# A tenth weight place for the experts, in the room of a smaller descriptor scratch, on one Trainium2 core

## The chip, the cores and the metric

The kernel runs on one core of one Trainium2 chip. The metric is the device time of one execution in microseconds (us); the median of three runs of the kernel before is 1637.58 us. A smaller number is better.

## The reference, cut to what matters

The work is two blocks on 256 tokens of width 1024, all in float32. The first block has two layers with retention, dilated attention, a gated mix and a feed-forward part of width 2816. The second has a state-space branch, a pooling branch and a mixture of 32 experts. The change touches how weights and small vectors arrive; the part whose weights it touches most is the mixture:

```python
MOE_EXPERTS = 32; MOE_TOP_K = 2; D_EXPERT = 512
def swiglu(xb, wg, wu, wd):
    return (jax.nn.silu(xb @ wg) * (xb @ wu)) @ wd
# each token goes to 2 of the 32 experts:
#   yb = swiglu(tokens of expert e, w_eg[e], w_eu[e], w_ed[e])
#   y  = sum over the token's experts of yb * gate weight
```

Each expert has three weights of 1024 x 512 (or 512 x 1024) float32 values, 2 MB (2,097,152 bytes) each, so 96 weights have to come from memory, 201 MB in all. All 32 experts are computed, each for at most 64 tokens.

## The kernel before, in words

The five engines run programs that are written out by hand, with semaphores between them. `weights()` makes one list of units of weights for both layers and the first part of the second block. SyncE (SP) loads them in order into the places of `ring` (four in the layers, two after), by `load_to(u)`, which waits until the unit that held the place has been split. ScalarE makes the high part of each quarter (`hi_to`), VectorE or GpSimd (POOL) the low part (`lo_to`), TensorE (PE) multiplies three times per quarter. PE signals `split_done`, and the splits of quarter k wait for it at quarter k - 4.

The stages follow each other: layer 0, layer 1, `convolution`, `scan` (32 steps over the 16 units called "merged"), `gates` (units "u", "branch_a", "branch_b", "out2"), `routing`, and then `experts`.

In `experts`, PE goes through 16 pairs of experts. For pair p it needs weights 6p to 6p + 5: two gate weights, two up weights, two down weights. `gate_up(p)` multiplies 64 columns for each expert of the pair with 512 columns of weights, `down(p)` does the product back. Weight k lies in `slot_for(0, k)`, which is `expert_slots[k % 9]`: four places in the arena, four in `ring`, one in `rows`, 2 MB each. Weights 0 to 7 are issued by ScalarE during `gates` as places come free. SP issues weight 8 when the last `out2` product has been read, and then, in `expert_loads(0, 8)`, the others in order: weight k waits until PE has signalled that it is done with weight k - 9 (`("gu", r, b, 0)` after the gate part, `("gu", r, b, 1)` after the up part, `("oe", r, b, 1)` after the down part). Weights 2, 9, 10 and the last four are loaded in halves (`half_load`). There are further rounds for experts with more than 64 tokens, behind a condition (`further`); they use eight places.

GpSimd issues small loads itself, 128 partitions wide as a rule: `c1`, `WS` (the gating weights, 128 x 4 runs of 512 bytes, at step k = 1 of each layer), `GB` (two gains, at k = 4), and at the very start `posi`, six pieces of `colrow`, two more, and then `GCOL`, `BCOL` (128 x 2 runs of 16 bytes each) and `BP` (128 x 4 runs of 16 bytes). A generator `small_loads()` holds 17 more. Two of them are issued at k = 8 of layer 0, the others one at a time after each `low(m)` of layer 0's steps m = 2 to 16; ten of those are the router's weights `WR` (128 x 4 short runs each). A step m of the feed-forward part is two quarters of weights: POOL makes `low(m)`, one low part of a quarter (the other is VectorE's), and this one load.

The descriptors of the loads that GpSimd issues lie in a scratch in the on-chip memory, at its default size in the kernel before (the argument `dynamic_dma_scratch_size` is not given).

Of the kernel before, what the change touches and what calls it, by code (L numbers as in the profile page):

```python
# [13 lines left out]
P = 128  # L14
D = 1024
# [276 lines left out]
def program(nc, A, out):  # L292
    st = ExitStack()
    with st:
# [24 lines left out]
        posi = sb("posi", [P, 2], I32)  # L319
        rope = sb("rope", [P, 2, 2, 32])  # L320
        rt = rows[:, 4 * D:4 * D + P].rearrange("p (a b c) -> p a b c", a=2, b=2)
        posf = sb("posf", [P, 2])
        cnt = sb("cnt", [P, 1], I32)
        AR = 26624
        ar_at = nc.sbuf_base + (-nc.sbuf_base) % 32
# [46 lines left out]
        s_last = {e: sem(f"last_{e}") for e in ("dve", "pool")}  # L372
        s_w = [[sem(f"expert{i}") for i in range(9)]] + [[sem(f"expert{r}_{i}") for i in range(8)] for r in range(1, ROUNDS)]
        s_second = [sem(f"expert_second{i}") for i in range(4)]
        s_round = [None] + [{e: sem(f"round{r}_{e}") for e in ("pe", "act", "dve")} for r in range(1, ROUNDS)]
# [55 lines left out]
        GT2 = view(23424, 2, 512)  # L431
        JUNK = view(25472, 2, 512)
        ACH = view(4096, 22, 256, rounded=True)
        ACL = view(9728, 22, 256, rounded=True)
# [53 lines left out]
        def blocks8(a0, a1, rounded=False):  # L488
# [43 lines left out]
        SEL, RK, CW, RS, CM, CB = R(400, 2, 32), R(464, 2, 32), R(528, 2, 32), R(592, 2, 32), R(656, 1, 2), R(660, 2, 36)  # L532
        expert_slots = [ar[:, 18432:18432 + SLOT], ar[:, 22528:22528 + SLOT], ar[:, 10240:10240 + SLOT], ar[:, 14336:14336 + SLOT],
                        ring[:, 0:SLOT], ring[:, SLOT:2 * SLOT], ring[:, 2 * SLOT:3 * SLOT], ring[:, 3 * SLOT:4 * SLOT], rows[:, D:D + SLOT]]

        slot_for = lambda r, k: expert_slots[k % (9 if r == 0 else 8)]

# [49 lines left out]

        in_halves = lambda r, k: r == 0 and (k in (2, 9, 10) or k >= 92)

        def half_load(e, k, q):  # L590

            p, j = divmod(k, 6)
            o = slot_for(0, k)[:, q * RAW:(q + 1) * RAW]
            w = A["w_expert_up_2" if j < 4 else "w_expert_down_2"][0, 2 * p + j % 2]
            src = w.rearrange("(q p k) n -> q p (k n)", q=2, k=4)[q] if j < 4 else w.rearrange("(p q k) n -> q p (k n)", q=2, k=2)[q]
            e.dma_start(o, src).then_inc(*landed(s_second[k % 4] if q else s_w[0][k % 9], ("ew", 0, k, q)))

        def tensor(t):  # L600
# [346 lines left out]
            def convolution():  # L947
# [17 lines left out]
                for m in range(24):  # L965
                    c = CHUNKS[m]
                    if m < 3:
                        finished(m + 1)
                    else:
                        bk = take(("cv", m), ("conv", m))  # L970
                        chunk(bk if c < 20 else bk[:, 256:512], q0 + 1 + m, 0 if c < 20 else 1, 2).then_inc(*sig(s_mm, ("cv", m), ("split_done", q0 + 1 + m)))
                    if m >= 2:
                        to_tokens(m - 2)
                    if m == 1:
                        bk = take(("dtt",), ("dtraw",))
                        t.wait_ge(*at("cv", -1, "kept"))
                        for i in range(4):
                            made = t.transpose(bk[:, i * 64:(i + 1) * 64], DTT[:, tok(i)], ident[0:64, 0:64])
                        made.then_inc(*sig(s_turn, ("dtt",)))
                    if m == 10:  # L980
                        dt_sums()
                    if m == 11:
                        bk = take(("acst",), ("acsr", 0), ("acsr", 1))
                        t.wait_ge(*at("acs"))
                        for i in range(4):
                            made = t.transpose(bk[:, tok(i)], ACS[:, i % 2, :], ident)
                        made.then_inc(*sig(s_turn, ("acst_t",)))
                    if m == 17:
# [12 lines left out]
                    if m in SUMMED:  # L1001
                        state_sum(SUMMED[m])
# [395 lines left out]
        def scalar(s):  # L1398
# [356 lines left out]
            def gates():  # L1755
                n0 = first["u",][1]
                for u in range(2):
# [4 lines left out]
                    if u == 0:  # L1762
# [11 lines left out]
                s.wait_ge(*at("sacc", 15))  # L1774
                expert_load(s, 0, 1)
                s.wait_ge(*at("ss", "kept"))
# [15 lines left out]
                for u in range(4):  # L1792
                    for a in range(2):
                        hi_to(n0 + 2 * u + a + 4)
                    if u >= 2:
                        s.wait_ge(*at("ba", 3))
                        half_load(s, 2, u - 2)
# [4 lines left out]
                expert_load(s, 0, 3)  # L1802
                s.wait_ge(*at("bb", 3, "kept"))
                expert_load(s, 0, 5)
                for n in range(1, 5):
                    s.wait_ge(*at("lo", len(quarters) - n))
                expert_load(s, 0, 4)
# [908 lines left out]
        def gpsimd(g):  # L2716
# [34 lines left out]
            def small_loads():  # L2751
# [13 lines left out]
                yield  # L2765
                for q in range(2):
                    rows_of = lambda x: x[512 * q:512 * q + 512].rearrange("(p k) n -> p k n", k=4)
                    g.dma_start(WR[:, 4 * q:4 * q + 4, 0:4], rows_of(A["w_router_group_2"][0])).then_inc(*landed(s_small[5]))
                    yield
                    for k in range(4):  # L2770
                        g.dma_start(WR[:, 4 * q:4 * q + 4, 4 + 8 * k:12 + 8 * k], rows_of(A["w_router_expert_2"][0, k])).then_inc(*landed(s_small[6]))
                        yield

            def layer(l):
# [9 lines left out]
                for k in range(28):  # L2784
                    lo_to(n0 + k + 4)
                    if k == 1:
                        g.wait_ge(*at("z", l, 0, 1))
                        g.wait_ge(*at("hl", j, 1, 1))
                        g.wait_ge(*at("hh", j, 1, 1))
                        g.dma_start(WS[:, :, :], A["w_s"][l].rearrange("g t s -> t g s")).then_inc(*landed(s_ws, ("ws_in", l)))  # L2790
                    if k == 4:
# [4 lines left out]
                    if k == 8 and l == 0:  # L2796
                        loads = small_loads()
                        next(loads), next(loads)
# [86 lines left out]
            g.dma_start(colrow[0:48, 2, :], fl(A["b_ada_2"][0])).then_inc(*landed(s_col[1]))  # L2885
            for o, name in ((GCOL, "ln1_g_2"), (BCOL, "ln1_b_2")):
                g.dma_start(fold(o, 2), A[name][0].rearrange("(q p k) -> p q k", q=2, k=4)).then_inc(*landed(s_col[3]))
            g.dma_start(fold(BP, 4), A["b_ada_2"][0][3 * D:5 * D].rearrange("(u p k) -> p u k", u=4, k=4)).then_inc(*landed(s_col[3], ("bp_in",)))
            layer(0)
# [73 lines left out]
        def sync(y):  # L2963
# [25 lines left out]
            def expert_loads(r, first_one):  # L2989

                n_slots = len(s_w[r])
                for k in range(first_one, 96):
                    if k >= n_slots and not (r == 0 and k in (9, 10)):
                        b, i = divmod(k - n_slots, 6)
                        y.wait_ge(*(at("gu", r, b, i // 2) if i < 4 else at("oe", r, b, 1)))
                    if not in_halves(r, k):
                        expert_load(y, r, k)
                    elif k == 10:
                        for q in range(2):
                            y.wait_ge(*at("gu", 0, 0, 0 if q else "first"))  # L3000
                            for x in (9, 10):
                                half_load(y, x, q)
# [5 lines left out]
            for l in range(2):  # L3008
# [5 lines left out]
                for m, u in ADA_AT[l].items():  # L3014
# [84 lines left out]
```

## Time and profile before

| what | value |
|---|---|
| median of 3 runs (lowest, highest) | 1637.58 us (1637.37, 1638.76) |
| span of the profiled execution, first to last instruction | 1635.8 us |
| TensorE busy, and its mean granted clock | 1585.8 us (97%), 0.995 |
| VectorE, ScalarE, GpSimd busy | 762.6, 611.0, 473.7 us |
| moved by DMA | 397.87 MB, mean 243 GB/s |

The span leaves out what lies ahead of the first and behind the last instruction, which is 1.8 us between the span and the median. Engine names in the rows: PE is TensorE's matmuls, PEld its weight loads, DVE VectorE, ACT ScalarE, POOL GpSimd, SP SyncE; a "q" behind one is its queue or sequencer. L145 and L151 are lines of helpers through which all matmuls and all two-tensor operations go, L171 is the one through which all loads go, so instructions are told apart by their tiles. Idle time of an engine stands in square brackets with what ended it.

### The profile page before, as it was taken

What the parts mean: (1) busy time and instruction counts of PE and PEld (TensorE: products, weight loads), DVE (VectorE), ACT (ScalarE), POOL (GpSimd) and SP (SyncE); (2) the same over time, 40 slices, a digit from 0 to 9 for tenths busy, and PEclk for the clock granted to TensorE, in tenths of its full rate; (3) what the DMA queues carried; (4) which work ended last, traced back from release to release, by engine and by line L of the source; (5) the groups of instructions that cost most, each with busy time, mean ns of one, the idle gap of its engine ahead of it and who ended that gap; (6) DMA issues with size and microseconds to landing.
All of it is one profiled execution on the core that took longest, in us unless ns stands there. A gap on an engine that the chain in (4) does not pass through costs nothing.

```text
span 1635.8 us, 24320 instructions
## 1 busy us (share of the span) xinstructions
PE 1585.8 (97%) x9881; PEld 1204.8 (74%) x9881; DVE 762.6 (47%) x1261; ACT 611.0 (37%) x1113; POOL 473.7 (29%) x305
## 2 busy tenths in 40 slices
PE   6999999999999999999999999999999999999997
PEld 5988899878889998888778888898644444444442
DVE  4554433246454332578776666446532323333223
ACT  4644444345544443555446665333211111111010
POOL 4342655433434444300036665343300000000000
PEclk9999999999999999999999999999999999999998
DMA  7654997546439986433313333957999999999995
GB/s 264 220 158 128 266 260 232 174 141 218 153 98 312 263 269 220 118 80 85 103 52 104 104 103 120 296 152 264 360 400 423 425 420 422 424 422 424 421 422 210
DMA packets 244757, 397.87 MB, mean 243 GB/s; under 512 B 6837, under 2 KB 195697, under 8 KB 223392
## 3 DMA queue, kind: packets, MB, share of 16 engines
q1 hardware_dynamic: 237840, 365.45, 64.6%
q10 hardware_dynamic: 3776, 20.85, 3.2%
q0 software_dynamic: 3024, 9.95, 1.8%
q8 instruction: 81, 1.33, 0.3%
q14 instruction: 36, 0.29, 0.1%
HBM read 395.17 MB, written 1.05 MB: 242 GB/s over the span
## 4 chain that ended last, share of the span: by engine, by line
PE 82%; DMA 9%; DVE 3%; issue 2%; ACT 2%; POOL 1%; ACTq 0%; DVEq 0%; POOLq 0%; SPq 0%
PE ps L145 80%; DMA arena<-in_w_expert_up 4%; DMA arena<-in_w_expert_gate 4%; PE ps L147 2%; DVE arena L151 1%; DVE arena L155 1%; DMA ring<-in_w_out 1%; POOL split_r L151 1%; ACT arena L149 1%; DMA X<-in_x 1%; ACT split_r L149 1%; DVE split_r L151 0%; DMA ring<-in_w_in 0%; POOL arena_r L151 0%; DVE X L155 0%
## 5 line engine op out<-in xcount | busy, mean ns | idle before, releaser
L145 PE MATMUL ps<-arena_r,split_r 128*128 128x256 f32 (+1 forms) x2984 | 459.9, 288 | 2.2 <-POOL split_r L151 2.2
L151 POOL TENSOR_TENSOR split_r<-ring,split_r 128x1024 fp32r<-128x1024 f32 (+1 forms) x142 | 329.3, 2320 | 304.2 <-ACT split_r L149 275.6
L145 PEld LDWEIGHTS ps<-arena_r,split_r 128*128 128x128 f32 x2984 | 393.3, 188 | 19.7 <-issue 13.6
L149 ACT ACTIVATE split_r<-ring 128x1024 fp32r<-128x1024 f32 (+1 forms) x293 | 295.7, 1019 | 265.2 <-PE ps L145 183.2
L151 DVE TENSOR_TENSOR split_r<-ring,split_r 128x1024 fp32r<-128x1024 f32 (+1 forms) x151 | 217.4, 1442 | 302.6 <-ACT split_r L149 302.4
L145 PE MATMUL ps<-split_r,arena_r 128*128 128x512 f32 (+1 forms) x1520 | 341.0, 378 | 4.1 <-POOL split_r L151 2.4
L145 PEld LDWEIGHTS ps<-split_r,arena_r 128*128 128x128 f32 x1520 | 276.1, 189 | 50.3 <-issue 7.1
L145 PE MATMUL ps<-arena 128*64 128x512 f32 (+8 forms) x1456 | 299.1, 461 | 6.3 <-DMA arena<-in_w_expert_gate 2.2
L145 PE MATMUL ps<-hhh_r,split_r 128*128 128x256 f32 (+1 forms) x976 | 221.7, 316 | 0.0
L145 PEld LDWEIGHTS ps<-arena 128*64 128x64 f32 (+2 forms) x1456 | 126.0, 148 | 129.7 <-issue 115.2
L145 PE MATMUL ps<-ring,arena 128*64 128x512 f32 (+2 forms) x768 | 211.4, 576 | 3.0 <-DMA ring<-in_w_expert_up 1.7
L149 ACT ACTIVATE arena<-ps 128x256 f32<-128x256 f32 (+4 forms) x175 | 75.4, 446 | 257.3 <-PE ps L145 215.3
L145 PEld LDWEIGHTS ps<-hhh_r,split_r 128*128 128x128 f32 x976 | 161.6, 188 | 12.5 <-issue 0.6
L151 DVE TENSOR_TENSOR arena<-arena,ps 128x512 f32<-128x512 f32 (+1 forms) x120 | 72.7, 634 | 202.9 <-PE ps L145 177.3
L145 PEld LDWEIGHTS ps<-ring,arena 128*64 128x64 f32 (+1 forms) x768 | 77.3, 144 | 98.8 <-issue 89.4
L171 POOL DMA_DIRECT2D rows<-in_ln_g x1 | 0.6, 617 | 412.2 <-PE ps L145 412.2
L149 ACT ACTIVATE arena<-ps,modc 128x128 f32<-128x128 f32 x80 | 30.0, 455 | 199.2 <-PE ps L145 198.5
L149 ACT ACTIVATE arena_r<-arena 128x512 fp32r<-128x512 f32 (+2 forms) x96 | 51.0, 540 | 138.5 <-DVE arena L155 86.9
L145 PEld LDWEIGHTS ps<-arena,X 128*128 128x128 f32 x640 | 77.4, 198 | 28.5 <-issue 26.4
L145 PE MATMUL ps<-arena,X 128*128 128x128 f32 x640 | 82.6, 284 | 14.6 <-DVE arena L153 14.6
L155 DVE SCALAR_TENSOR_TENSOR arena<-ps,rows,arena 128x508 f32<-128x508 f32 (+4 forms) x104 | 69.7, 675 | 28.5 <-ACT arena L149 21.9
L151 POOL TENSOR_TENSOR arena_r<-arena,arena_r 128x256 fp32r<-128x256 f32 (+1 forms) x46 | 38.1, 830 | 151.3 <-ACT arena_r L149 143.7
(164 smaller groups left out, 1234.0 us busy)
## 6 DMA issues: line engine op xcount, KB each, us to landing
ring<-in_w_gate_up SPq DMA_DIRECT2D x88, 512.0 KB, 7.4
arena<-in_w_expert_gate SPq DMA_DIRECT2D x15, 2048.0 KB, 27.9
ring<-in_w_in SPq DMA_DIRECT2D x57, 512.0 KB, 5.3
ring<-in_w_expert_gate SPq DMA_DIRECT2D x13, 2048.0 KB, 25.7
ring<-in_w_expert_down SPq DMA_DIRECT2D x13, 2048.0 KB, 28.5
arena<-in_w_ada SPq DMA_DIRECT2D x24, 1024.0 KB, 7.4
arena<-in_w_expert_up SPq DMA_DIRECT2D x12, 2048.0 KB, 25.1
ring<-in_w_down SPq DMA_DIRECT2D x22, 1024.0 KB, 4.9
```

Source lines behind the costliest of these rows:

```text
L145: made = e.matmul(*a, **k)
L147: made = e.transpose(*a, **k)
L149: made = e.activation(*a, **k)
L151: made = e.tensor_tensor(*a, **k)
L155: made = e.scalar_tensor_tensor(**k)
L171: made = e.dma_start(*a, **k)
```

## The change

1. `dynamic_dma_scratch_size=512` is given: the descriptors' scratch takes 512 bytes of each partition. In the room there is a new tensor `tenth` of 2 MB. The small table `rope` moves into the arena.
2. `expert_slots` has ten places in the first round, `tenth` being the first. Weight k lies in place k % 10. What ScalarE issued as weights 0 to 7 it now issues as weights 1 to 8, at the same points and into the same places. Weight 0 is issued by SP in the scan, after eight units of "merged", and goes into `tenth`. After the last `out2` product SP issues weight 9, and weight k then waits until PE is done with weight k - 10. The weights in halves are now 3, 10, 11 and the last four.
3. GpSimd's loads of 512 runs are each cut in two of 256: `WS` is loaded at k = 1 and k = 3 of each layer, `BP` in two, each `WR` load in two (20 in place of 10). `GCOL`, `BCOL` and `BP` move from the start into the generator, ahead of `WR`. The generator now holds 31 loads; two are issued at k = 8 of layer 0, and one after each `low(m)` in both layers: 20 in layer 0 (m = 2 to 21), 9 in layer 1 (m = 2 to 10).

```diff
-        rope = sb("rope", [P, 2, 2, 32])
+        tenth = sb("tenth", [P, SLOT])
...
+        rope = ar[:, 26496:26624].rearrange("p (a b c) -> p a b c", a=2, b=2)
...
-        expert_slots = [ar[:, 18432:18432 + SLOT], ar[:, 22528:22528 + SLOT], ...
+        expert_slots = [tenth[:, :], ar[:, 18432:18432 + SLOT], ar[:, 22528:22528 + SLOT], ...
-        slot_for = lambda r, k: expert_slots[k % (9 if r == 0 else 8)]
+        slot_for = lambda r, k: expert_slots[k % (10 if r == 0 else 8)]
-        in_halves = lambda r, k: r == 0 and (k in (2, 9, 10) or k >= 92)
+        in_halves = lambda r, k: r == 0 and (k in (3, 10, 11) or k >= 92)
...
-                        t.wait_ge(s_small[5], 32)
-                        t.wait_ge(s_small[6], 128)
+                        t.wait_ge(s_small[5], 64)
+                        t.wait_ge(s_small[6], 256)
...
-                        expert_load(s, 0, 0)
+                        expert_load(s, 0, 1)
...
-                expert_load(s, 0, 6)
                 expert_load(s, 0, 7)
+                expert_load(s, 0, 8)
...
+                for o, name in ((GCOL, "ln1_g_2"), (BCOL, "ln1_b_2")):
+                    g.dma_start(fold(o, 2), ...)
+                    yield
+                for x in range(2):
+                    g.dma_start(fold(BP, 4)[:, 2 * x:2 * x + 2, :], ...)
+                    yield
-                for q in range(2):
+                for q in range(4):
                     (one load of WR[:, 2q:2q+2, 0:4], four of WR[:, 2q:2q+2, 4+8k:12+8k], a yield after each)
...
-                        g.dma_start(WS[:, :, :], A["w_s"][l].rearrange("g t s -> t g s")).then_inc(...)
+                    if k in (1, 3):
+                        x = k // 2
+                        g.dma_start(WS[:, 2 * x:2 * x + 2, :], A["w_s"][l, 2 * x:2 * x + 2].rearrange("g t s -> t g s")).then_inc(...)
...
-                    if l == 0:
-                        next(loads, None)
+                    next(loads, None)
...
-            for o, name in ((GCOL, "ln1_g_2"), (BCOL, "ln1_b_2")):
-                g.dma_start(fold(o, 2), ...)
-            g.dma_start(fold(BP, 4), ...)
...
+            load_to(first["merged",][0] + 8)
+            expert_load(y, 0, 0)
             load_to(first["end",][0])
             y.wait_ge(*at("o2", 1, 1, "kept"))
-            expert_loads(0, 8)
+            expert_loads(0, 9)
...
-    nc = bacc.Bacc("TRN2", target_bir_lowering=False, num_devices=1)
+    nc = bacc.Bacc("TRN2", target_bir_lowering=False, num_devices=1, dynamic_dma_scratch_size=512)
```

## Rows read from the trace of the kernel before

**Rows 1.** The page: busy time, and GB/s in 40 slices of the span.

```profile
PE 1585.8 (97%) x9881; PEld 1204.8 (74%) x9881; DVE 762.6 (47%) x1261; ACT 611.0 (37%) x1113; POOL 473.7 (29%) x305
...
GB/s 264 220 158 128 266 260 232 174 141 218 153 98 312 263 269 220 118 80 85 103 52 104 104 103 120 296 152 264 360 400 423 425 420 422 424 422 424 421 422 210
```

**Rows 2.** Windows: stretch, its length, busy time of each engine, clock, DMA share, GB/s.

```profile
890.00:960.00 70.00, 70.00 (x541) 60.85 (x538) 42.95 (x88) 42.99 (x98) 41.53 (x23) 1.00 0.40 105
...
1172.00:1196.00 24.00, 24.00 (x146) 11.43 (x144) 6.71 (x12) 4.79 (x11) 7.72 (x6) 1.00 0.91 346
1196.00:1423.00 227.00, 227.00 (x1230) 104.81 (x1228) 74.38 (x135) 30.19 (x73) 0.00 (x0) 1.00 1.01 420
1423.00:1612.00 189.00, 179.75 (x950) 84.92 (x946) 56.37 (x97) 22.78 (x55) 1.14 (x2) 1.00 1.01 421
```

**Rows 3.** Waits of PE from 1160 to 1636: us in total, times, longest.

```profile
PE ps L145 <- DMA ring<-in_w_expert_gate: 3.3, 3, 1.3
PE ps L145 <- DMA arena<-in_w_expert_gate: 2.2, 2, 1.2
PE ps L145 <- DMA arena<-in_w_expert_up: 2.0, 3, 0.8
...
PE ps L145 <- DMA ring<-in_w_expert_up: 1.7, 2, 0.9
```

**Rows 4.** Timeline of PE in the experts: start, us, idle before it.

```profile
1473.40 0.61 PE L145 MATMUL ps<-arena 128*64 128x512 f32 x1 [0.99 <-DMA ring<-in_w_expert_gate]
...
1592.89 7.09 PE L145 MATMUL ps<-arena 128*64 128x512 f32 x32 [1.23 <-DMA arena<-in_w_expert_gate]
```

**Rows 5.** Timeline of SP's queue as the experts start.

```profile
1172.56 0.34 SPq L171 DMA_DIRECT2D arena<-in_w_expert_up  x1
...
1195.95 0.38 SPq L171 DMA_DIRECT2D ring<-in_w_expert_gate  x1
```

**Rows 6.** The chain that ended last, its piece at 1592.89.

```profile
1592.89 18.24 PE ps L145 x76
```

**Rows 7.** The scan: SP's loads from 899 on, and one of ScalarE's splits.

```profile
899.11 31.36 SPq L171 DMA_DIRECT2D ring<-in_w_in  x8
...
920.52 1.05 ACT L149 ACTIVATE split_r<-ring 128x1024 fp32r<-128x1024 f32 x1
```

**Rows 8.** Timeline of POOL, feed-forward steps: with a load, without, and layer 1.

```profile
219.80 0.74 POOL L151 TENSOR_TENSOR arena_r<-arena,arena_r 128x256 fp32r<-128x256 f32 x1 [1.95 <-ACT arena_r L149]
220.49 0.77 POOL L171 DMA_DIRECT2D small<-in_w_router_expert  x1
...
225.65 0.73 POOL L151 TENSOR_TENSOR arena_r<-arena,arena_r 128x256 fp32r<-128x256 f32 x1 [1.95 <-ACT arena_r L149]
...
271.67 0.74 POOL L151 TENSOR_TENSOR arena_r<-arena,arena_r 128x256 fp32r<-128x256 f32 x1 [2.42 <-ACT arena_r L149]
...
277.43 0.73 POOL L151 TENSOR_TENSOR arena_r<-arena,arena_r 128x256 fp32r<-128x256 f32 x1 [2.41 <-ACT arena_r L149]
...
502.21 2.39 POOL L151 TENSOR_TENSOR split_r<-ring,split_r 128x1024 fp32r<-128x1024 f32 x1 [0.21 <-ACT split_r L149]
506.55 0.74 POOL L151 TENSOR_TENSOR arena_r<-arena,arena_r 128x256 fp32r<-128x256 f32 x1 [1.94 <-ACT arena_r L149]
```

**Rows 9.** Timeline of PE as the feed-forward steps start: layer 0, layer 1.

```profile
169.03 3.11 PE L145 MATMUL ps<-arena_r,split_r 128*128 128x256 f32 x24 [0.83 <-POOL split_r L151]
...
502.56 6.01 PE L145 MATMUL ps<-arena_r,split_r 128*128 128x256 f32 x48
```

**Rows 10.** POOL's loads: KB each, median us from issue to landing.

```profile
arena<-in_w_s POOLq DMA_DIRECT2D x2, 256.0 KB, 7.0
...
small<-in_w_router_expert POOLq DMA_DIRECT2D x8, 16.0 KB, 5.8
```

**Rows 11.** Timeline of POOL behind the gains' loads at k = 4, layer 0 and layer 1.

```profile
43.03 1.84 POOL L151 TENSOR_TENSOR split_r<-ring,split_r 128x768 fp32r<-128x768 f32 x1 [1.75 <-ACT split_r L149]
...
378.68 1.83 POOL L151 TENSOR_TENSOR split_r<-ring,split_r 128x768 fp32r<-128x768 f32 x1 [4.90 <-ACT split_r L149]
```

More of the change, by code:

```diff
@@ L372, in program @@
         s_last = {e: sem(f"last_{e}") for e in ("dve", "pool")}
-        s_w = [[sem(f"expert{i}") for i in range(9)]] + [[sem(f"expert{r}_{i}") for i in range(8)] for r in range(1, ROUNDS)]
-        s_second = [sem(f"expert_second{i}") for i in range(4)]
+        s_w = [[sem(f"expert{i}") for i in range(10)]] + [[sem(f"expert{r}_{i}") for i in range(8)] for r in range(1, ROUNDS)]
+        s_second = [sem(f"expert_second{i}") for i in range(5)]
         s_round = [None] + [{e: sem(f"round{r}_{e}") for e in ("pe", "act", "dve")} for r in range(1, ROUNDS)]
@@ L532, in program @@
         SEL, RK, CW, RS, CM, CB = R(400, 2, 32), R(464, 2, 32), R(528, 2, 32), R(592, 2, 32), R(656, 1, 2), R(660, 2, 36)
-        expert_slots = [ar[:, 18432:18432 + SLOT], ar[:, 22528:22528 + SLOT], ar[:, 10240:10240 + SLOT], ar[:, 14336:14336 + SLOT],
+        expert_slots = [tenth[:, :], ar[:, 18432:18432 + SLOT], ar[:, 22528:22528 + SLOT], ar[:, 10240:10240 + SLOT], ar[:, 14336:14336 + SLOT],
                         ring[:, 0:SLOT], ring[:, SLOT:2 * SLOT], ring[:, 2 * SLOT:3 * SLOT], ring[:, 3 * SLOT:4 * SLOT], rows[:, D:D + SLOT]]
-        slot_for = lambda r, k: expert_slots[k % (9 if r == 0 else 8)]
+        slot_for = lambda r, k: expert_slots[k % (10 if r == 0 else 8)]
         ADA_AT = ({4: 0, 8: 1, 12: 2, 16: 3, 20: 4}, {3: 5, 6: 6, 9: 7, 12: 8, 15: 9, 18: 10, 20: 11})
@@ L595, in half_load @@
             src = w.rearrange("(q p k) n -> q p (k n)", q=2, k=4)[q] if j < 4 else w.rearrange("(p q k) n -> q p (k n)", q=2, k=2)[q]
-            e.dma_start(o, src).then_inc(*landed(s_second[k % 4] if q else s_w[0][k % 9], ("ew", 0, k, q)))
+            e.dma_start(o, src).then_inc(*landed(s_second[k % 5] if q else s_w[0][k % 10], ("ew", 0, k, q)))
         def tensor(t):
@@ L1774, in gates @@
                 s.wait_ge(*at("sacc", 15))
-                expert_load(s, 0, 1)
+                expert_load(s, 0, 2)
                 s.wait_ge(*at("ss", "kept"))
@@ L1796, in gates @@
                         s.wait_ge(*at("ba", 3))
-                        half_load(s, 2, u - 2)
+                        half_load(s, 3, u - 2)
                     s.wait_ge(*at("mt", u))
@@ L1801, in gates @@
                 s.wait_ge(*at("bb", 3))
-                expert_load(s, 0, 3)
+                expert_load(s, 0, 4)
                 s.wait_ge(*at("bb", 3, "kept"))
-                expert_load(s, 0, 5)
+                expert_load(s, 0, 6)
                 for n in range(1, 5):
                     s.wait_ge(*at("lo", len(quarters) - n))
-                expert_load(s, 0, 4)
+                expert_load(s, 0, 5)
                 s.wait_ge(*at("o2", 1))
-                expert_load(s, 0, 6)
                 expert_load(s, 0, 7)
+                expert_load(s, 0, 8)
             def routing():
@@ L2765, in small_loads @@
                 yield
-                for q in range(2):
-                    rows_of = lambda x: x[512 * q:512 * q + 512].rearrange("(p k) n -> p k n", k=4)
-                    g.dma_start(WR[:, 4 * q:4 * q + 4, 0:4], rows_of(A["w_router_group_2"][0])).then_inc(*landed(s_small[5]))
+                for o, name in ((GCOL, "ln1_g_2"), (BCOL, "ln1_b_2")):
+                    g.dma_start(fold(o, 2), A[name][0].rearrange("(q p k) -> p q k", q=2, k=4)).then_inc(*landed(s_col[3]))
+                    yield
+                for x in range(2):
+                    g.dma_start(fold(BP, 4)[:, 2 * x:2 * x + 2, :], A["b_ada_2"][0][(3 + x) * D:(4 + x) * D].rearrange("(u p k) -> p u k", u=2, k=4)).then_inc(
+                        *landed(s_col[3], *([("bp_in",)] if x else [])))
+                    yield
+                for q in range(4):
+                    rows_of = lambda x: x[512 * (q // 2):512 * (q // 2) + 512].rearrange("(p k) n -> p k n", k=4)[:, 2 * (q % 2):2 * (q % 2) + 2, :]
+                    g.dma_start(WR[:, 2 * q:2 * q + 2, 0:4], rows_of(A["w_router_group_2"][0])).then_inc(*landed(s_small[5]))
                     yield
                     for k in range(4):
-                        g.dma_start(WR[:, 4 * q:4 * q + 4, 4 + 8 * k:12 + 8 * k], rows_of(A["w_router_expert_2"][0, k])).then_inc(*landed(s_small[6]))
+                        g.dma_start(WR[:, 2 * q:2 * q + 2, 4 + 8 * k:12 + 8 * k], rows_of(A["w_router_expert_2"][0, k])).then_inc(*landed(s_small[6]))
                         yield
+            loads = small_loads()
             def layer(l):
@@ L2789, in layer @@
                         g.wait_ge(*at("hh", j, 1, 1))
-                        g.dma_start(WS[:, :, :], A["w_s"][l].rearrange("g t s -> t g s")).then_inc(*landed(s_ws, ("ws_in", l)))
+                    if k in (1, 3):
+                        x = k // 2
+                        g.dma_start(WS[:, 2 * x:2 * x + 2, :], A["w_s"][l, 2 * x:2 * x + 2].rearrange("g t s -> t g s")).then_inc(
+                            *landed(s_ws, *([("ws_in", l)] if x else [])))
                     if k == 4:
@@ L2796, in layer @@
                     if k == 8 and l == 0:
-                        loads = small_loads()
                         next(loads), next(loads)
@@ L2885, in gpsimd @@
             g.dma_start(colrow[0:48, 2, :], fl(A["b_ada_2"][0])).then_inc(*landed(s_col[1]))
-            for o, name in ((GCOL, "ln1_g_2"), (BCOL, "ln1_b_2")):
-                g.dma_start(fold(o, 2), A[name][0].rearrange("(q p k) -> p q k", q=2, k=4)).then_inc(*landed(s_col[3]))
-            g.dma_start(fold(BP, 4), A["b_ada_2"][0][3 * D:5 * D].rearrange("(u p k) -> p u k", u=4, k=4)).then_inc(*landed(s_col[3], ("bp_in",)))
             layer(0)
@@ L2992, in expert_loads @@
                 for k in range(first_one, 96):
-                    if k >= n_slots and not (r == 0 and k in (9, 10)):
+                    if k >= n_slots and not (r == 0 and k in (10, 11)):
                         b, i = divmod(k - n_slots, 6)
@@ L2997, in expert_loads @@
                         expert_load(y, r, k)
-                    elif k == 10:
+                    elif k == 11:
                         for q in range(2):
                             y.wait_ge(*at("gu", 0, 0, 0 if q else "first"))
-                            for x in (9, 10):
+                            for x in (10, 11):
                                 half_load(y, x, q)
```

## The prediction

> **What bounds the kernel now.** First the page. PE is busy 1585.8 of 1635.8 us, and from about slice 30 of 40 on the GB/s stand at 420 to 425 until the last slice [rows 1]. So the kernel has one limit for most of its time, PE, and may have a second one at the end, where the experts' weights come in. Second, the windows over the experts' stage [rows 2]. From 1172 to 1196 the DMA engines move 346 GB/s, with gaps. From 1196 on they are full, at 420 and 421 GB/s. PE is full as well until 1423 (227.00 of 227), and then no longer: 179.75 of 189 us. The reader is to see that the stage begins as PE's and ends as the memory's. Third, PE's waits in this stage [rows 3]: ten waits for an expert's weight, 3.3 + 2.2 + 2.0 + 1.7 = 9.2 us in all, which is what the third window lacks (189 - 179.75 = 9.25). Fourth, the timeline of PE [rows 4] says how the last part goes: the gate weights of one pair let PE go on at 1473.40 and those of the pair four later at 1592.89. That is 24 loads in 119.49 us, 4.98 us each, or 29.9 us a pair. A weight is 2.097 MB, and 2.097 MB at 421 GB/s are 4.98 us too. Behind the last such wait PE works without a gap for 18.24 us [rows 6].
>
> So two bounds for the end of this stage lie close together. One is the memory: from 1196 on every weight that is still to come costs 4.98 us. The other is PE's own work, which would end 9.2 us earlier than it does.
>
> **The change, part by part.** *The tenth place.* Which loads have to come in the full stretch decides. Before, weights 9 to 95 are issued from 1172.56 on, as PE gives places back, and from 1195.95 on the queue does not run dry [rows 5]. After, PE gives its places back at the same times, since nothing before it is changed, but the weight that goes into each is one further on: what 1172.56 issues is weight 10. The pattern of issues and the gaps ahead of 1196 stay, and each weight lands when its predecessor in the list did. In the stretch that the memory sets, that is 4.98 us sooner. All ten waits of PE are on such weights, so each wait's end moves by 4.98 us or the wait goes. The end moves by the smaller of 4.98 and 9.2 us: -4.98. I take it whole, because what is left of the waits, 4.2 us, says that memory still ends last. The waits used up first are those that came first, four or five of the ten; the last, at 1592.89, comes at about 1587.9, with the same 18.24 us and the closing norm behind it.
>
> *Where the 2 MB of weight 0 go.* SP issues weight 0 right behind the eighth unit of the scan, which its two loads at 899.11 begin [rows 7]. The stretch from 890 to 960 moves 105 GB/s at a share of 0.40 [rows 2], so there is room for five us of transfer. The queue is in order, so the ninth unit stands behind it. SP issues a unit about every ten us (four begin within 31.36 us [rows 7]), so the ninth near 909; by then most of the 2.5 + 5.0 us of the eighth unit and the weight have passed, and some 2 us of it may still stand ahead. The ninth unit's first split is the one at 920.52 [rows 7] (two splits a unit, and SP issues it when the two of the seventh are through), so it has over 5 us in hand. If it still made PE wait, PE would lose at most the weight's 5 us. Cost: 0, bounds 0 and +5.
>
> *ScalarE's loads* keep points, places and number: 0. *`rope` in the arena*: the same operations on the same engines, 0.
>
> *POOL's loads.* Issues added: 1 for `WS` in each layer, 1 for `BP`, 10 for `WR`: 13, of which each takes POOL 0.77 us [rows 8], 10 us of an engine that is busy 473.7 of 1635.8 [rows 1]. What matters is the place. In a step of layer 0 POOL has a load behind `low(m)` already, and it still idles 1.95 us until ScalarE is ready; a step with a load takes 225.65 - 219.80 = 5.85 us, one without 277.43 - 271.67 = 5.76 us, and PE is full in both. Five more steps of layer 0 (m = 17 to 21) and nine of layer 1 get one. At 0.09 us each that would be +1.3 us if it reached PE, at 0 if it does not; PE's matmuls follow each other without a gap in both kinds of step, so I take 0. The place where it can reach PE is the first step. At 169.03 PE waits 0.83 us for POOL's low part behind the first load of layer 0 [rows 9]. In layer 1 the low part ends at 502.21 + 2.39 = 504.60; the 48 products that begin at 502.56 use it from their 25th on, half of 6.01 us later, at 505.5. A load of 0.77 us fills 0.21 us of idle time and makes it 0.56 us later, 505.2. Slack of 0.3 us is left: 0, bound +0.6.
>
> *The smaller scratch.* This has no row: nothing in the trace of before waits for room for descriptors. A lower bound is 0. The upper one I take from landings: if a load of 256 runs can't be issued before the one ahead has landed, POOL stands with the low parts queued behind the load, and VectorE and PE behind them. In layer 0 a landing takes 5.8 us [rows 10] and a step 5.85, so there is no wait. In the first steps of layer 1 a step takes 5.3 us (506.55 less 502.21 is 4.34, and `low` and 0.21 us of idle lie ahead of 502.21) and the wait would be 0.5 us; POOL idles 1.94 us in it. At k = 4 two gain loads follow the second part of `WS` closely. With 7.0 us for its landing [rows 10], POOL could be held up for some 2 to 3 us; the idle time before its next low part is 1.75 us in layer 0 and 4.90 us in layer 1 [rows 11]. I take 0, and +1 as the upper bound of this together. The Trainium skill ("DMA: Bandwidth & Descriptors", The descriptor swizzle and Terms) gives 16 bytes for a descriptor and nine of them per engine for a load with one run per partition. By that, 512 bytes hold 32 per engine, a load of 256 runs needs 17, two of them do not fit together, and one of 512 runs would not fit at all. No row here shows it; it is why the bound above is not left out, and it leaves the sum as it is.
>
> *GCOL, BCOL, BP later.* They are first read in layer 1's modulation and after; they leave the start, where POOL waits for others: 0.
>
> Sum: -4.98 + 0 + 0 + 0 = -4.98 us. Against the profiled execution this makes a span of 1635.8 - 5.0 = 1630.8. The median lies 1.8 us above that span, so the time is 1637.58 - 4.98 = 1632.6 us.
>
> **The rivals.** *A: POOL's loads become a bound (slower).* Place: the 29 steps with a load. The next load is let in only some time x after the one before has landed, so a step can't be shorter than 5.8 + x. About 17 of the 29 steps are short ones (5.3 to 5.9 us; the others hold modulation products). With x = 1 us they lose about 1 us each, 17 us, and the time is 1632.6 + 17 = 1649.6. It eats the gain from x = 0.3 us on. For it: landing and step are so near each other. Against it: the 1.95 us that POOL idles in such a step, which would hide a part of x that this sum counts in full. By the skill's numbers above the condition for it, one load at a time, is there; by them alone x is not known, and at x = 0 the time stays 1632.6.
>
> *B: the gain is paid elsewhere (same).* The 2 MB in the scan make the ninth unit late and PE waits for it, or the full memory was not what ended last. The first gives back up to 5 us: 1637.6. Against it: the 105 GB/s, and no wait of PE in that window. Against the second: the ten waits. This is also the rival that the change does not do what it says.
>
> *C: the gain is cut by half (faster or same).* POOL's loads cost PE 1 to 3 us at the two layers' starts: 1633.6 to 1635.6. Above 1634.3 it counts as the same.
>
> **How the numbers follow.** The measurement can tell 0.2%, 3.3 us, from no change. Chances: forecast 0.70, C 0.14 (two thirds of it faster by over 0.2%), B 0.08, A 0.08. Faster 0.70 + 0.09 = 0.79, same 0.05 + 0.08 = 0.13, slower 0.08. The likeliest case's own range is 1631.6 to 1634.0: a load may be worth 0.5 us more or less, and the two small bounds at POOL add to 1.3. The range of 8 in 10 reaches from 1631.0 into C, to 1635.8.
>
> **What would show it.** Windows over the experts: the stretch at 420 GB/s ends near 1607 in place of 1612, PE's waits for weights sum to about 4.2 us and begin after 1513 in place of before 1473. Right for the scan: still no wait for loads there, GB/s up in one 10 us stretch. Right for POOL: steps of 5.8 us with loads in both layers, and experts starting at the same time. Wrong: a start of the experts that is later than before by more than 1 us; a span of POOL's load far over 0.77 us (it stands for room); low parts that PE waits for in the layers.

## The result, and the profile after

The changed kernel takes 1633.18 us in the median of 20 runs (1628.12 to 1636.13). The kernel before, timed beside it on the same chip, takes 1637.32 us in the median of 20 (1631.97 to 1641.69). The ratio is 0.9971, with a 95% interval of 0.9962 to 0.998. It is faster by 0.29%, more than the 0.2% that the prediction took as the grain. The predicted time was 1632.6 us, 0.6 us below the measured median.

The page of the kernel after, the lines that answer to [rows 1]:

```profile
span 1627.6 us, 24333 instructions
PE 1584.1 (97%) x9881; PEld 1202.5 (74%) x9881; DVE 770.8 (47%) x1261; ACT 610.8 (38%) x1113; POOL 481.6 (30%) x318
...
GB/s 265 214 157 129 261 269 223 183 129 229 149 85 318 263 262 225 121 89 103 81 76 104 156 104 105 306 134 243 389 389 422 426 420 422 424 422 424 422 422 213
```

This one profiled execution is 8.2 us shorter than that of the kernel before (1635.8), about twice what the medians say; with its 1629.42 us it is 3.8 us under the median of its own kernel. So the first reading has to be: which part of the 8.2 us belongs to the change?

The windows over the experts' stage, which answer to [rows 2]; the columns are the same, with the granted clock, DMA share and GB/s last:

```profile
1172.00:1196.00 24.00, 24.00 (x146) 11.46 (x144) 9.36 (x18) 5.42 (x12) 4.69 (x4) 1.00 0.91 359
1196.00:1423.00 227.00, 227.00 (x1228) 105.37 (x1226) 73.44 (x131) 30.16 (x73) 0.00 (x0) 1.00 1.01 423
1423.00:1604.00 181.00, 176.21 (x938) 81.51 (x934) 54.88 (x95) 22.18 (x54) 1.15 (x2) 1.00 1.01 421
```

PE's waits for experts' weights, 1150 to 1636, which answer to [rows 3], and three of the five places where they stand in PE's timeline, which answer to [rows 4]:

```profile
PE ps L145 <- DMA rows<-in_w_expert_gate: 1.1, 1, 1.1
PE ps L145 <- DMA ring<-in_w_expert_gate: 1.0, 1, 1.0
PE ps L145 <- DMA arena<-in_w_expert_gate: 1.0, 1, 1.0
...
PE ps L145 <- DMA arena<-in_w_expert_up: 0.8, 1, 0.8
PE ps L145 <- DMA ring<-in_w_expert_up: 0.8, 1, 0.8
```

```profile
1525.32 0.61 PE L145 MATMUL ps<-ring,arena 128*64 128x512 f32 x1 [1.14 <-DMA rows<-in_w_expert_gate]
1535.28 0.61 PE L145 MATMUL ps<-tenth,arena 128*64 128x512 f32 x1 [0.83 <-DMA arena<-in_w_expert_up]
...
1584.77 0.61 PE L145 MATMUL ps<-tenth,arena 128*64 128x512 f32 x1 [0.99 <-DMA arena<-in_w_expert_gate]
```

The reader is to see that the third window still runs at 421 GB/s, that PE now lacks 181 - 176.21 = 4.8 us there and not 9.25, and that five waits of the ten are left, 4.7 us in all. The first comes at 1525.32; before, they had begun ahead of 1473. The experts' stage, from PE's first gather product to the end of the span, is 1627.6 - 1160.49 = 467.1 us long; before it was 1635.8 - 1163.76 = 472.0. That is 4.9 us. The other 3.3 us were gained ahead of the stage, and the experiments say whose they are.

A second way to count leaves out the first microseconds of the stage. SP's first load into a place that PE gives back needs the same signal of PE in both kernels; it is issued at 1172.56 before ([rows 5]) and at 1169.55 after. From there to the end of the span it is 463.2 us before and 458.1 after. In the 26.5 us behind it the DMA engines move 9.0 MB in both kernels: the gaps did stay what they were, as the prediction assumed.

### The profile page after: what moved, and what is told of

Its sections match the earlier page's. It is cut to its first block, busy times and chain, and to the rows that moved or that the text cites. A ratio compares the mean times of both kernels' runs of the same rounds, so it can differ in the third digit from the quotient of the medians.

```text
span 1627.6 us, 24333 instructions
## 1 busy us (share of the span) xinstructions
PE 1584.1 (97%) x9881; PEld 1202.5 (74%) x9881; DVE 770.8 (47%) x1261; ACT 610.8 (38%) x1113; POOL 481.6 (30%) x318
## 3 DMA queue, kind: packets, MB, share of 16 engines
HBM read 395.17 MB, written 1.05 MB: 243 GB/s over the span
## 4 chain that ended last, share of the span: by engine, by line
PE 85%; DMA 7%; DVE 3%; ACT 2%; issue 1%; POOL 1%; SPq 0%; ACTq 0%; DVEq 0%; POOLq 0%
PE ps L145 83%; DMA arena<-in_w_expert_gate 2%; DMA arena<-in_w_expert_up 2%; PE ps L147 2%; DMA ring<-in_w_out 1%; DVE arena L155 1%; DVE arena L151 1%; POOL split_r L151 1%; DMA X<-in_x 1%; ACT arena L149 1%; ACT split_r L149 1%; DVE split_r L151 1%; DMA ring<-in_w_gate_up 1%; DMA ring<-in_w_in 0%; POOL arena_r L151 0%
## 5 line engine op out<-in xcount | busy, mean ns | idle before, releaser
L151 DVE TENSOR_TENSOR split_r<-ring,split_r 128x1024 fp32r<-128x1024 f32 (+1 forms) x151 | 226.3, 1501 | 296.9 <-ACT split_r L149 296.7
L145 PE MATMUL ps<-arena 128*64 128x512 f32 (+8 forms) x1392 | 319.1, 454 | 2.3 <-DMA ring<-in_w_expert_gate 1.0
L145 PE MATMUL ps<-ring,arena 128*64 128x512 f32 (+2 forms) x688 | 225.3, 574 | 2.0 <-DMA rows<-in_w_expert_gate 1.1
L145 PEld LDWEIGHTS ps<-arena 128*64 128x64 f32 (+2 forms) x1392 | 129.9, 149 | 117.1 <-issue 102.0
```

The lines of the kernel that those rows point to most:

```text
L145: made = e.matmul(*a, **k)
L151: made = e.tensor_tensor(*a, **k)
```

## Experiments

Four kernels ran on one chip (e1 to e4), four on a second (e5 to e8), two on a third (e9 and e10). The kernel before had medians of 1637.95, 1638.45 and 1635.57 us there; ratios are to it. The changed kernel ran on the second and third chip too (e5, e10), but not on the one of e1 to e4. "The stage" is the experts' stage, counted as above from PE's first gather product.

**e1 and e2: all of the change but the tenth place.** Nine places as before, and no weight 0 in the scan, with POOL's loads split and spread as in the changed kernel; e1 has the 512 bytes of scratch, e2 the default. Against the changed kernel, cut:

```diff
-        tenth = sb("tenth", [P, SLOT])
...
-        slot_for = lambda r, k: expert_slots[k % (10 if r == 0 else 8)]
+        slot_for = lambda r, k: expert_slots[k % (9 if r == 0 else 8)]
...
-            load_to(first["merged",][0] + 8)
-            expert_load(y, 0, 0)
```

In e2 also:

```diff
-    nc = bacc.Bacc("TRN2", target_bir_lowering=False, num_devices=1, dynamic_dma_scratch_size=512)
+    nc = bacc.Bacc("TRN2", target_bir_lowering=False, num_devices=1)
```

> Nine places as before, but POOL's loads cut and spread as in the change, with the scratch of 512 bytes: the change without its tenth place. Theory (the whole gain is the one load less in the stretch that memory sets): no change, ratio to before 0.9995 to 1.0010, PE's waits for experts' weights 9 to 10 us in sum, and 0.3 us of POOL's waiting after a landing hidden. Rival A (POOL's waits for room reach PE): slower by 1 to 5 us, ratio 1.0006 to 1.003. Rival D (the change at POOL brings part of the gain, since the experts started 3 us earlier in the profile of after): faster by 2 to 3 us.

> Nine places, POOL's loads cut and spread as in the change, but the default scratch. Theory: same as before, within 1 us, and no idle time ahead of a POOL load that ends 0.3 us after a landing. If the small scratch costs anything, this one is faster than its twin with 512 bytes by that much; the theory says under 0.5 us.

Measured: e1 1638.05 us, ratio to before 1.0004 (0.9991 to 1.0018); e2 1636.84 us, 0.9994 (0.9982 to 1.0005). Their stages are 471.9 and 471.6 us long, as that of before. PE's waits in e1's experts:

```profile
PE ps L145 <- DMA ring<-in_w_expert_gate: 3.0, 3, 1.0
PE ps L145 <- DMA arena<-in_w_expert_gate: 2.8, 2, 1.8
PE ps L145 <- DMA arena<-in_w_expert_up: 2.3, 3, 0.8
PE ps L145 <- DMA ring<-in_w_expert_up: 1.7, 2, 0.9
```

They sum to 9.8 us, against 9.2 before. What follows: POOL's loads and the scratch together neither cost nor give anything that these runs can tell. e2 is 1.2 us faster than e1 where under 0.5 was expected, which is inside the scatter (drawing the runs anew gives -0.3 to 2.7 us, 95%). The gain is the tenth place's, with the early load of weight 0 that it allows.

**e3 and e4: the changed kernel with less to load.** One weight (20) or three (20, 26, 32) are loaded as 64 KB in place of 2 MB; PE's work is all there, with data that are not the experts' in those places. The lines of e4:

```diff
+            if r == 0 and k in (20, 26, 32):
+                o, src = slot_for(r, k)[:, 0:128], w.rearrange("(p k) n -> p (k n)", k=w.shape[0] // P)[:, 0:128]
```

> The changed kernel with the load of weight 20 (a down... or up weight in the full stretch) cut to its first 64 KB, so that one more load of 2 MB is missing in that stretch. Theory (memory and PE lie 4.7 us apart after the change): the time falls by 4.7 us against the changed kernel, the sum of PE's waits for weights goes to about 0, and the kernel is 8.5 to 10 us below the one before. Rival (a load is worth 4.98 us and the next bound is far): falls by 5.0 as well, so this run alone does not tell; with the next one it does.

> The changed kernel with the loads of weights 20, 26 and 32 cut to their first 64 KB each. Theory: PE's own work is the bound from the first cut load on, so the same time as with one cut load, 4.7 us below the changed kernel, waits for weights 0. Rival (memory alone sets the end): 15 us below the changed kernel.

Measured: e3 1627.16 us, 0.993 (0.9915 to 0.9945), with 1.8 us of waits for weights and a stage of 464.9 us. e4: 1625.89 us, 0.9926 (0.9911 to 0.9941), no such wait, a stage of 460.9 us. The two waits left in e3, from PE's timeline:

```profile
1563.72 7.09 PE L145 MATMUL ps<-ring,arena 128*64 128x512 f32 x32 [0.79 <-DMA ring<-in_w_expert_up]
1583.46 0.61 PE L145 MATMUL ps<-tenth,arena 128*64 128x512 f32 x1 [0.97 <-DMA arena<-in_w_expert_gate]
```

The medians are 10.8 and 12.1 us under that of before, where 8.5 to 10 was expected of e3 and the same time as e3's of e4. With 2 MB less, the waits did not go to about 0.

What follows: e4 shows PE's own bound. Nothing waits for memory in it, and its stage ends 5.7 us before the mean of the ten-place kernels (466.5, below) and 10.9 before that of the nine-place ones (471.8). Their waits, 4.3 to 4.7 and 9.2 to 9.8 us, say less than that. The rest is in PE's busy time from SP's load of the second count on: 442.5 us before, with ten waits, 441.9 after, with five, 441.1 in e4. A wait costs PE a little more than its idle time, some 0.15 us each as an estimate from these three.

e3 is less clear. Its PE began the stage more slowly: from 1160.27 on the granted clock was at half (1.2 GHz) for 6.8 us, in the profile of after for 3.4. So PE gave its first place back 10.2 us after its first gather product and not 9.1. The third last column is the granted clock, after first, then e3:

```profile
1160.00:1165.00 5.00, 4.50 (x26) 4.54 (x27) 1.14 (x5) 0.00 (x0) 0.00 (x0) 0.66 1.01 425
1165.00:1170.00 5.00, 5.00 (x29) 2.22 (x29) 0.59 (x1) 1.50 (x4) 4.25 (x4) 1.00 0.72 300
```

```profile
1160.00:1165.00 5.00, 4.10 (x21) 3.91 (x21) 1.15 (x7) 0.00 (x0) 0.00 (x0) 0.53 1.02 429
1165.00:1170.00 5.00, 5.00 (x27) 3.48 (x28) 1.38 (x2) 1.50 (x4) 3.27 (x3) 0.79 0.82 342
```

Counted from SP's first load into a place given back, which leaves this out, the ten-place kernels take 458.0 to 458.1 us, e3 454.8 and e4 452.6. One load less is worth 3.2 us by that count and not 4.98. Of the 1.8 us lacking, about 1 is in the bytes: in the first 150 us of that count the DMA engines move 0.3 to 0.5 MB less than in the ten-place kernels (0.7 to 1.1 us at 421 GB/s), so a part of the room that the missing load leaves stays unused. The rest is open. The picture of two bounds holds: with one load less two waits are left, with three none. That a load is worth 4.98 us is not shown by e3.

**e5 and e10: the changed kernel again,** each as the reference of the kernels on its chip. No edit.

> The changed kernel once more, for a second profile of it and as the partner of the next three on one chip. Theory: 4 to 5.5 us below the one before; the start of the experts lies at 1169 to 1174 us and differs from profile to profile by up to 3 us, which is not the change's doing.

> The changed kernel, for the comparison with the kernel of halves. Its median is 4 to 5 us under that of the kernel before, the experts' stage 466 to 467.2 us long, and PE's waits on expert loads 4 to 5 us. If the place is worth what the product of one load and the stage's length say, the ratio is 0.996 to 0.9975.

Measured: e5 1630.01 us, 0.9957 (0.994 to 0.9975), stage 466.3 us, waits 4.3 us; that is 8.4 us under the one before, where 4 to 5.5 was expected. e10 1631.17 us, 0.9976 (0.9963 to 0.999), stage 466.2 us, waits 4.6 us. With the first comparison the medians are 4.1, 8.4 and 4.4 us under those of before; the mean of the three ratios, 0.9968, is 5.2 us. The stage is 471.8 us in the mean of the three nine-place profiles (before, e1, e2) and 466.5 in that of the three ten-place ones: 5.3 us. By the second count it is 463.2, 463.6 and 463.3 us against 458.1, 458.0 and 458.0: 5.4 us, and no profile of one kind comes near the other.

**e6 and e9: more bytes ahead of the full stretch.** The changed kernel, and in addition weights 12 to 15 come in halves, since PE gives the places of the first pair back by halves; for that, PE takes the first pair's down products half by half too.

```diff
-        in_halves = lambda r, k: r == 0 and (k in (3, 10, 11) or k >= 92)
+        in_halves = lambda r, k: r == 0 and (k in (3, 10, 11, 12, 13, 14, 15) or k >= 92)
...
+                    elif k in (13, 15):
+                        for q in range(2):
+                            y.wait_ge(*(at("gu", 0, 0, 1 if q else "third") if k == 13 else at("oe", 0, 0, 1 if q else "first")))
...
```

> The changed kernel, with weights 12 to 15 in halves too: the places of the first pair are given back half by half, so that the queue does not run dry near 1182 and 1194 (two gaps of 1.7 us of transfer each in the profile of after). Theory (every us of the memory's time in that stretch counts until PE's own bound, 4.7 us away, is reached): 3.4 us below the changed kernel. Rival (the gaps do not count because they only move): the same as the changed kernel.

> The kernel that gives the places of pair 0 back by halves, so that weights 12 to 15 come in halves, a second time, with the changed kernel beside it on the same chip. Theory A (the bytes moved in the stretch where places are short set the end of the experts' stage): the profile again has about 405 GB/s between 1170 and 1196 us where the changed kernel has about 340, the experts' stage is 464 to 465 us long against 466 to 467, and the median is 1.5 to 2.5 us under that of the changed kernel. Theory B (the 0.5 us between the two medians before was the scatter of the runs): the two medians agree within 0.8 us although the stage in the profile is shorter.

Measured: e6 1629.51 us, 0.9946 (0.993 to 0.9963), stage 464.1 us, waits 2.7 us. e9 1627.54 us, 0.9954 (0.9939 to 0.997), stage 465.6 us, waits 4.6 us. Windows of the stretch in which places are short, first the changed kernel, then e6, then e9:

```profile
1170.00:1196.00 26.00, 26.00 (x154) 12.12 (x152) 9.36 (x18) 5.42 (x12) 6.69 (x6) 1.00 0.90 343
```

```profile
1170.00:1196.00 26.00, 26.00 (x154) 12.13 (x152) 9.38 (x18) 5.43 (x12) 5.79 (x5) 1.00 0.99 407
```

```profile
1170.00:1196.00 26.00, 26.00 (x156) 12.31 (x155) 9.73 (x18) 5.42 (x12) 4.64 (x4) 1.00 1.01 416
```

What follows: the gaps are filled in both runs, and both spans, 1624.5 and 1625.0 us, are under all three of the ten-place kernel (1627.3 to 1628.0). PE's last wait for a weight ends at 1581.62 and 1582.05, in the ten-place kernels at 1584.53 to 1585.02. The medians are 0.5 and 3.6 us under the changed kernel's on the same chip, where 3.4 and then 1.5 to 2.5 was expected; the mean times are 1.8 and 3.7 us under it. Drawing the runs anew gives 1.2 to 4.3 us for the mean of the two (95%), but for e6 alone it reaches 0. So this version is the fastest that does all the work, by 1 to 4 us. Some of the gain is given back: from 1196 to 1250 e6 and e9 move 415 and 414 GB/s, the changed kernel 425. e9's stage is 465.6 us and not 464 to 465, it still waits 4.6 us, and by the second count only e6 is shorter (455.9 us, e9 458.2). That does not speak against the version: PE was 1.1 us ahead at the stage's start (1159.36 against 1160.49 after) and saw no low clock in it, while the DMA engines were full (416 GB/s), so more of the same memory time shows up as waiting. This last is a reading of one profile. A sum of waits says how far PE is ahead of the loads, not when the loads end.

**e7 and e8: the second half of weight 3 later.** The theory was that this half delays the last `out2` unit, for which PE had waited before the experts. The half is issued behind weight 4; e7 does it to the changed kernel, e8 to that of halves.

```diff
-                        half_load(s, 3, u - 2)
+                        if u == 2:
+                            half_load(s, 3, 0)
...
                 expert_load(s, 0, 4)
+                half_load(s, 3, 1)
```

> The changed kernel, with the second half of weight 3 issued by ScalarE 11 us later, behind the split of the last out2 unit, so that it does not lie ahead of that unit's load. Theory: the last out2 unit lands up to 1.5 us sooner and the experts start 1 to 2 us earlier; the 1 MB goes into the full stretch, costs up to 2.5 us there, of which the 2.7 us gap near 1169 takes most: together 0 to 2 us below the changed kernel. Rival (memory sets the end, so 1 MB more in its stretch costs in full): 0 to 2.5 us above it.

> Both edits of the two runs before. Theory: their sum, 3.4 to 5.4 us below the changed kernel and 8 to 10 us below the one before.

Measured: e7 1633.15 us, 0.9958 (0.9939 to 0.9977), stage 469.3 us; e8 1631.36 us, 0.9956 (0.9938 to 0.9973), stage 469.1 us. e7's wait at the last `out2` products was the longest of all twelve profiles:

```profile
1139.42 10.12 PE L145 MATMUL ps<-split_r,arena_r 128*128 128x512 f32 x36 [2.99 <-POOL split_r L151]
```

The theory is not borne out: e7 began the stage 2.4 us later than e5, and e8, which waited 0.72 us there, only 0.2 us earlier than e6. Both stages are long, by 2.7 us against the ten-place kernels and by 4.2 against e6 and e9 (464.9). That is not the price of 1 MB in the full stretch alone: in both profiles the granted clock was at half for 6.8 us at the stage's start, against 3.4 us in the changed kernel and e6 and none in e9. By the second count e7 is 1.0 us longer than the ten-place kernels, and e8 (458.9) 3.0 longer than e6 (455.9) and 0.7 longer than e9 (458.2). The medians are 3.1 us (e7) and 1.4 us (e8) above e5's, but e7's ratio is that of e5. What the edit costs stays open; it gives nothing.

## Why the prediction was right

**What bounds the kernel: right.** e1 and e2 keep nine places and keep the time; e3 and e4 take bytes away and the waits go. The memory's bound is where the prediction put it. PE's lies 10.9 us under it (471.8 less 460.9) and not 9.2: the sum of the waits undercounts what PE gets back when they go. Since only 4.98 of it was used, the forecast did not depend on this.

**The tenth place, -4.98 us: right.** The stage became 4.9 us shorter in the first pair of profiles and 5.3 us in the mean of three against three (5.4 by the second count), inside the half microsecond that the prediction allowed a load. The mechanism and its size are so borne out. That the time itself came within 0.6 us is in part luck: the interval of the ratio reaches from 3.3 to 6.2 us, and one of the three comparisons gave 8.4. The waits left are 4.3 to 4.7 us (predicted 4.2), five of ten, the earliest gone first. The last wait ends at 1584.77, 3.1 us before the 1587.9 predicted, because the stage began 3.3 us earlier.

**Weight 0 in the scan, 0 us: right.** SP's queue there:

```profile
899.47 0.99 SPq L171 DMA_DIRECT2D ring<-in_w_in  x2
900.51 1.28 SPq L171 DMA_DIRECT2D tenth<-in_w_expert_gate  x1
908.73 0.99 SPq L171 DMA_DIRECT2D ring<-in_w_in  x2
```

The weight lands at 911.29, 10.8 us after its issue and later than the prediction's five us of transfer, but the ninth unit lands at 914.77 against 914.22 before, and PE waits for no load there. Rival B's first form is out by this, its second by e3 and e4.

**POOL's loads, 0 us: right, and the mechanism of rival A is real.** POOL's timeline in layer 1, with steps in which it stands for room (the idle time before an instruction is in brackets):

```profile
513.21 0.74 POOL L151 TENSOR_TENSOR arena_r<-arena,arena_r 128x256 fp32r<-128x256 f32 x1 [1.95 <-ACT arena_r L149]
514.52 0.73 POOL L171 DMA_DIRECT2D small<-in_w_router_expert  x1 [0.56 <-issue]
515.27 2.38 POOL L151 TENSOR_TENSOR split_r<-ring,split_r 128x1024 fp32r<-128x1024 f32 x1
519.61 0.75 POOL L151 TENSOR_TENSOR arena_r<-arena,arena_r 128x256 fp32r<-128x256 f32 x1 [1.95 <-ACT arena_r L149]
520.87 0.73 POOL L171 DMA_DIRECT2D small<-in_w_router_expert  x1 [0.52 <-issue]
```

Nothing that POOL works on is missing in the 0.56 us. The load before landed at 514.205, and this one goes 0.32 us later; the next pair is 520.562 and 520.87, and in layer 0 it is 246.638 and 246.95, 266.933 and 267.24. So x, which the prediction had left open, is 0.31 to 0.33 us, and in these places one load at a time was let in. The Trainium skill ("DMA: Bandwidth & Descriptors", The descriptor swizzle and Terms) has the descriptor counts from which the prediction had worked out that two such loads don't fit; the trace agrees. At k = 4 it happens to the second of the two gain loads: it goes 0.33 us after the second part of `WS` has landed (41.625 and 375.262), two loads ahead of it, and POOL idles 1.05 us in layer 0 and 2.27 us in layer 1,

```profile
40.34 0.56 POOL L171 DMA_DIRECT2D rows<-in_g_mix_post  x1
41.95 0.55 POOL L171 DMA_DIRECT2D rows<-in_g_ffn_post  x1 [1.05 <-issue]
43.37 1.84 POOL L151 TENSOR_TENSOR split_r<-ring,split_r 128x768 fp32r<-128x768 f32 x1 [0.87 <-ACT split_r L149]
```

and in layer 0 the idle time before the next low part falls from the 1.75 us of [rows 11] to 0.87: it paid for the wait. That the small scratch is the cause is shown by e2: it has the same 55 loads and the default scratch, and POOL idles ahead of none of them in this way. All ten kernels with 512 bytes show it, e1 too (0.90 us at k = 4 of layer 0, 2.39 in layer 1). The same place in e2:

```profile
40.96 0.57 POOL L171 DMA_DIRECT2D rows<-in_g_mix_post  x1
41.53 0.55 POOL L171 DMA_DIRECT2D rows<-in_g_ffn_post  x1
```

By rival A's sum, which eats the gain from x = 0.3 us on, this x would have cost all of it. It cost nothing: PE's waits on POOL from 0 to 800 us are 0.9 us, 0.8 before, and e1 stands at 1.0004. What the sum left out is that PE sets the pace. Forty-eight products take 6.01 us ([rows 9]), POOL's steps with a load in layer 1 5.8 us (527.46 to 533.24, 533.24 to 539.04), where the first four had been 5.3 without. Two steps, those in which POOL stood for room, took 6.4 us (508.87 to 515.27 to 521.63), more than PE's 6.01. All this came out of POOL's lead, not PE's time. The first low part of layer 1 ends at 503.06 + 2.40 = 505.46; it is needed at 502.89 + 3.01 = 505.9.

**The 3.3 us ahead of the stage: not in the prediction, and not the change's.** PE's timeline of the last `out2` products, before and after:

```profile
1139.08 10.21 PE L145 MATMUL ps<-split_r,arena_r 128*128 128x512 f32 x36 [2.40 <-POOL split_r L151]
```

```profile
1137.35 8.66 PE L145 MATMUL ps<-split_r,arena_r 128*128 128x512 f32 x36 [0.41 <-POOL split_r L151]
```

The last `out2` unit took 6.24 us to land in the profile of before and 4.76 in that of after. PE waited 2.0 us longer and then did the same 36 products in 10.21 us in place of 8.66: 3.5 us together; the rest of the program ahead of them is 0.3 us longer in the kernel after. e5 and e10 waited 1.19 and 0.38 us, the nine-place e1 and e2 both 0.79, so the wait does not follow the number of places. (e7, with ten, waited 2.99, but its edit is at this very spot.) The low clock needs a second look: each of the three nine-place profiles has one such fall ahead of the stage (at 1139 us, and in e1 and e2 near 374), of the nine ten-place profiles only e7 has one. Over all runs there is hardly such a difference. The mean granted clock is 0.9958 in the nine runs of e5 and 0.9955 in the fifteen of the kernel before beside them, and 0.9959 in both for e10; one more fall in each run would show as 0.001. So it goes with the execution. Together with the stage: 3.5 - 0.3 + 4.9 = 8.1 of the 8.2 us.

## What to carry to other kernels

When a stage is memory's to its end, one more buffer is worth what it lets move ahead of the full stretch: its bytes divided by the full rate, up to what the other engine waits. Filling a gap works the same way (e6, e9), less what the full stretch then moves less. When two profiles differ by more than the medians, compare the stage of the change from its own first instruction to its end, or better from the first event behind which both kernels do the same, and look in further profiles of the same kernels at the waits that differ ahead of it. A rival that makes a helper engine slower has to be priced against the engine that sets the pace, not against the helper's own step.

## What the runs showed of the hardware

The granted clock of TensorE falls to half (1.2 GHz) for some 3.4 us in places, and not in every execution. Windows around the last `out2` products, before and after (the third last column is the granted clock):

```profile
1135.00:1140.00 5.00, 2.60 (x11) 1.79 (x10) 2.51 (x1) 2.00 (x2) 2.34 (x1) 0.93 0.67 233
1140.00:1145.00 5.00, 5.00 (x18) 3.98 (x17) 1.28 (x3) 0.00 (x0) 0.00 (x0) 0.73 1.05 446
```

```profile
1135.00:1140.00 5.00, 4.59 (x21) 3.41 (x19) 2.58 (x1) 0.68 (x1) 2.20 (x1) 1.00 0.98 351
1140.00:1145.00 5.00, 5.00 (x23) 4.03 (x22) 4.50 (x6) 0.00 (x0) 0.00 (x0) 1.00 0.99 421
```

The means 0.93 and 0.73 are (0.07 + 0.27) x 5 us x 2 = 3.4 us at half. Here it came in the two profiles in which PE had waited 2.40 and 2.99 us, where the 36 products took 10.21 and 10.12 us, and in none of the ten with waits of 0.38 to 1.26 us (8.66 to 8.68 us). A wait's length does not settle it everywhere: between the layers, PE waits 1.04 and 1.72 us around three products in the kernel after and the clock stays at 1.00; it waits 1.24 and 1.60 us in e1, and 1.01 and 1.76 us in e2, and in both the clock falls to half during the second wait and stays there for 3.4 us, which costs such a run 1.7 us. The windows from 375 to 380, of the kernel after and of e1:

```profile
375.00:380.00 5.00, 5.00 (x31) 4.96 (x30) 3.42 (x8) 1.70 (x2) 1.53 (x2) 1.00 0.91 293
375.00:380.00 5.00, 4.96 (x22) 4.96 (x23) 4.22 (x10) 1.34 (x2) 0.56 (x2) 0.72 0.97 329
```

At the start of the experts' stage, around 1160 us, the clock falls in eleven of the twelve profiles: for 3.4 us in eight, for 6.8 us in e3, e7 and e8, and not at all in e9. Each such fall moves a single profile by about as much as a third of this change's gain. What tips it where the waits are alike stays open.

The other is POOL's issue with a scratch of 512 bytes: a load that finds no room goes 0.31 to 0.33 us after the landing of the load ahead that frees it, which is the one before it or, at k = 4, the one before that.
